# Lag kernels of a state-space phase laid out by DMA within SBUF, into two buffers, instead of through DRAM

## The reference

```python
def step(h, u_blk):
    bu = jnp.einsum('btgn,gpn->btgp', u_blk.astype(jnp.complex64), bbar)
    bu = bu.at[:, 0].add(abar[None] * h)
    a = jnp.broadcast_to(abar, bu.shape)
    _, hs = lax.associative_scan(_linrec_combine, (a, bu), axis=1)
    y = jnp.einsum('btgp,gnp->btgn', hs, cmat).real
    return hs[:, -1], y
...
y = d * u                      # and, for rev in (0, 1): y = y + y_dir
g = jax.nn.gelu(y); out = g * sigmoid(g @ w + bias)
```

## Time and profile before

| | |
|---|---|
| median of 3 runs | 1737.36 us (1733.51 to 1750.48) |
| the profiled execution, its own time | 1738.68 us |
| its span in the profile | 1736.9 us |
| PE busy | 1546.6 us, 89% of the span |
| PE busy, 560 to 920 us | 291.1 of 360 us |
| PE busy, 1200 to 1737 us | 511.4 of 537 us |

### The profile page before, as it was taken

How to read it: one execution, slowest core, us unless ns; L and a number is a source line. 1 busy time by engine, 2 the same in 40 slices (tenths; PEclk the granted TensorE clock), 3 DMA queues, 4 the chain that set the end, 5 groups by cost and what they waited for, 6 DMA issues and landing times. The chain is left out here.

```text
span 1736.9 us, 28020 instructions
## 1 busy us (share of the span) xinstructions
PE 1546.6 (89%) x11286; PEld 1321.5 (76%) x11286; DVE 981.4 (57%) x1271; ACT 806.1 (46%) x1096; POOL 661.2 (38%) x507
## 2 busy tenths in 40 slices
PE   4799999799698899888658988888999999899998
PEld 0378888588687788778648976677999967689997
DVE  6444522488745277755724646564766655556665
ACT  2422222455413577665454434554554454455452
POOL 0088887599798924563741013311000010110000
PEclk8889999999899999887878999998999999899999
DMA  9966666355535677776657455314544333245541
GB/s 390 425 245 226 225 228 250 131 195 188 216 110 202 158 241 217 240 222 173 188 131 277 161 193 207 146 49 153 207 198 193 145 112 145 89 155 218 200 162 49
DMA packets 118713, 332.72 MB, mean 192 GB/s; under 512 B 30772, under 2 KB 72116, under 8 KB 102344
## 3 DMA queue, kind: packets, MB, share of 16 engines
q1 hardware_dynamic: 115734, 305.63, 49.8%
q10 hardware_dynamic: 2868, 25.54, 4.1%
HBM read 290.55 MB, written 40.58 MB: 191 GB/s over the span
## 5 line engine op out<-in xcount | busy, mean ns | idle before, releaser
L3018 PE MATMUL ffn_ps<-ffn_x_lead,w_lead 128*128 128x256 f32 x672 | 188.5, 280 | 1.1 <-DVE w_rest L3097 1.1
L3018 PE MATMUL ffn_ps<-ffn_x_lead,w_rest 128*128 128x256 f32 x672 | 188.7, 281 | 0.0
L3018 PE MATMUL ffn_ps<-ffn_x_rest,w_lead 128*128 128x256 f32 x672 | 188.5, 281 | 0.0
L401 POOL TENSOR_TENSOR w_rest<-resident_ring,w_lead 128x2048 fp32r<-128x2048 f32 x7 | 32.1, 4579 | 396.5 <-ACT w_lead L397 206.3
L3097 DVE TENSOR_TENSOR w_rest<-resident_ring,w_lead 128x2048 fp32r<-128x2048 f32 x42 | 96.1, 2292 | 83.7 <-ACT w_lead L3062 83.7
L365 PE MATMUL qkvz_ps<-qkvz_w_lead,h_lead 128*128 128x512 f32 x320 | 125.9, 393 | 5.4 <-POOL h_rest L646 5.4
L3018 PEld LDWEIGHTS ffn_ps<-ffn_x_lead,w_lead 128*128 128x128 f32 x672 | 126.2, 188 | 2.2 <-issue 1.5
L3018 PEld LDWEIGHTS ffn_ps<-ffn_x_rest,w_lead 128*128 128x128 f32 x672 | 126.5, 188 | 0.7
L3018 PEld LDWEIGHTS ffn_ps<-ffn_x_lead,w_rest 128*128 128x128 f32 x672 | 126.3, 188 | 0.0
L365 PE MATMUL qkvz_ps<-qkvz_w_lead,h_rest 128*128 128x512 f32 x320 | 125.5, 392 | 0.0
L365 PE MATMUL qkvz_ps<-qkvz_w_rest,h_lead 128*128 128x512 f32 x320 | 125.5, 392 | 0.0
(11 more groups left out here) (518 smaller groups left out, 4526.0 us busy)
## 6 DMA issues: line engine op xcount, KB each, us to landing
resident_ring<-in_ffn_gu SPq DMA_DIRECT2D x22, 2048.0 KB, 9.0
ffn_wd<-in_ffn_down SPq DMA_DIRECT2D x22, 1024.0 KB, 4.8
resident_ring<-in_ada_w SPq DMA_DIRECT2D x8, 2048.0 KB, 13.8
xc<-s_q_scratch SPq DMA_DIRECT2D x128, 128.0 KB
resident_x<-in_s_bT SPq DMA_DIRECT2D x64, 256.0 KB
resident_ring<-in_attn_w_in ACTq DMA_DIRECT2D x8, 2048.0 KB, 10.5
s_W_scratch<-resident_x SPq DMA_DIRECT2D x64, 256.0 KB, 3.3
resident_ring<-in_s_w SPq DMA_DIRECT2D x32, 512.0 KB, 8.3
```

Of the source, the lines that this page charges most:

```text
L401: self.core.nc.gpsimd.tensor_tensor(self.slots[1][0], self._raw(r), self.slots[0][0].bitcast(F32), ALU.subtract).then_inc(self.rest_made, 1)
L3018: last = nc.tensor.matmul(ps[s][f][:, m, :], w_part[w][m][:, k, f * P:(f + 1) * P], x_part[x][:, k, :], start=(k, w, x) == (0, 0, 0), stop ...
```

## The change

- `lags` no longer goes to DRAM. ACT, right behind its lag copy and a wait for its completion, issues four DMAs from SBUF to SBUF, one for each `j` (a 32-partition row of groups), which read the windows out of `lags` and write `T`. For tile 0 it waits there for the spill of `x` and the transposes that read `core.x`; for tiles from 2 on it waits for `outputs(kl-2)`.
- `T` has two buffers, `core.x` half and a new `T_odd`. The lag copy waits for the landing of the tile before's windows, as `lags` is single.
- The windows want (channel, step) order in the partitions of `T`. So `us` is stored without a permutation, `ub` is loaded in (channel, step) order, and the rows of `s5_W` follow: the access patterns of L1383 and L1385 swap the two.
- `b_fw`, `b_bw` and `direct` go. `lag_kernels` reads the half of the partitions of `b_all` and `V` that it needs, all backward products first, then the middle ones, then, behind a wait for the backward ones (`behind_done`), the forward ones.
- SP's list is reordered: the load of `ub` with its wait for the store comes early in the turn, the loads of weight tiles behind it.

```diff
@@ InputWeights.load
-                         ap=[[2 * P, CH], [0, SG], [1, 2 * P]]
+                         ap=[[0, SG], [2 * P, CH], [1, 2 * P]]
-                         ap=[[0, CH], [SN * 2 * P, SG], [1, WB * 2 * P]]
+                         ap=[[SN * 2 * P, SG], [0, CH], [1, WB * 2 * P]]
@@ s5_mixer
-        T = core.x[:, 0, :].rearrange("p (j m q) -> p j m q", j=4, q=2)
+        T_odd = ph.sb("T_odd", [P, DM])
+        T_raw = [m.rearrange("p (j m) -> p j m", j=4) for m in (core.x[:, 0, :], T_odd[:])]
+        T = [m.rearrange("p j (m q) -> p j m q", q=2) for m in T_raw]
-            return bass.AP(tensor=lagged.tensor, offset=lagged.offset + k * 2 * SG * CG * LAGW, ap=[[2 * SG, CH], [2 * LAGW, SG * 4], [1, 2 * P]])
+        def shifted(j):
+            return bass.AP(tensor=lags_at.tensor, offset=lags_at.offset + 32 * j * 2 * LAGW, ap=[[2 * LAGW, SG], [2 * SG, CH], [1, 2 * P]])
@@ SP
-                        sp.dma_start(bass.AP(tensor=to.tensor, offset=to.offset, ap=[[CH * NCH, CG], [CG * CH * NCH, SG], [1, CH * NCH]]), us[(n - 1) % 2][:]).then_inc(u_stored[(n - 1) % 2], 16)
+                        sp.dma_start(d["u"][n - 1], us[(n - 1) % 2][:].rearrange("p t n -> p (t n)")).then_inc(u_stored[(n - 1) % 2], 16)
-                        sp.wait_ge(l_kept, kl + 1)
-                        sp.dma_start(bass.AP(tensor=of.tensor, offset=of.offset, ap=[[LAGW * 2, 4], [4 * LAGW * 2, 2 * SG], [1, LAGW * 2]]),
-                                     lags[:].rearrange("m w q -> m (w q)")).then_inc(lag_stored, 16)
-                        sp.wait_ge(lag_stored, 16 * (kl + 1))
-                        sp.wait_ge(y_done, kl)
-                        sp.dma_start(core.x[:, 0, :].rearrange("p (j m) -> p j m", j=4), windows(kl)).then_inc(T_landed, 16)
@@ PE, lag_kernels and outputs
-                    pe.wait_ge(b_copied, k + 1)
+                    pe.wait_ge(b_landed[s], 16 * (k // 2 + 1))
-                    pe.wait_ge(T_landed, 16 * (k + 1))
+                    pe.wait_ge(T_landed[k % 2], 64 * (k // 2 + 1))
@@ ACT
                         if kl:
-                            act.wait_ge(lag_stored, 16 * kl)
+                            act.wait_ge(T_landed[(kl - 1) % 2], 64 * ((kl - 1) // 2 + 1))
                         act.wait_ge(l_done, kl + 1)
                         sc.activation(lags[:].rearrange("p w q -> p q w"), ps_l[:], ACT.Copy).then_inc(l_kept, 1)
+                        if kl == 0:
+                            act.wait_ge(spilled, 16)
+                            act.wait_ge(mod.turned, KT)
+                        act.wait_ge(l_kept, kl + 1)
+                        if kl >= 2:
+                            act.wait_ge(y_done, kl - 1)
+                        for j in range(4):
+                            act.dma_start(T_raw[kl % 2][:, j], shifted(j)).then_inc(T_landed[kl % 2], 16)
-                            direct(m)
-                    if 2 <= kl + 1 < CT:
-                        direct(kl + 1)
```

More of the change, by code:

```diff
@@ L1548, in s5_mixer @@
         ptab = ph.sb("ptab", [P, 2, CH, 2, QG])
-        b_all, b_fw, b_bw = [ph.sb(n, [P, 2, 2, CPAD]) for n in ("b_all", "b_fw", "b_bw")]
+        b_all = ph.sb("b_all", [P, 2, 2, CPAD])
         cc = ph.sb("cc", [P, 4, 2, P])
@@ L1569, in s5_mixer @@
         y_done, y_kept, turned, g_made, cleared, feed_made = [sem(n) for n in "y_done y_kept turned g_made cleared feed_made".split()]
-        lag_stored, T_landed, g_stored, z_stored, feed_in = [sem(n) for n in "lag_stored T_landed g_stored z_stored feed_in".split()]
+        g_stored, z_stored, feed_in = [sem(n) for n in "g_stored z_stored feed_in".split()]
+        T_landed = [sem(f"T_landed{s}") for s in range(2)]
         ub_landed = [sem(f"ub_landed{s}") for s in range(3)]
@@ L1574, in s5_mixer @@
         c_landed, V_landed = [[sem(f"{n}{s}") for s in range(4)] for n in ("c_landed", "V_landed")]
-        b_copied = sem("b_copied")
+        behind_done = sem("behind_done")
         LOADED = EarlyQuads.TILES
@@ L1714, in _ @@
                 g = nc.gpsimd
-                for b in (b_all, b_fw, b_bw):
-                    g.memset(b[:], 0.0).then_inc(cleared, 1)
+                g.memset(b_all[:], 0.0).then_inc(cleared, 1)
                 mod.rests(pool)
@@ L1770, in lag_kernels @@
                         pe.wait_ge(feed_made, 1)
+                    out = lambda j, q, cols: ps_l[32 * j:32 * j + 32, q, cols]
+                    at = lambda j, q: slice((4 * q + j) * SG, (4 * q + j) * SG + 32)
                     for q in range(2):
-                        r = 2 * k + q
-                        out = lambda j, cols: ps_l[32 * j:32 * j + 32, q, cols]
-                        at = lambda j: slice((4 * q + j) * SG, (4 * q + j) * SG + 32)
                         for c in range(2):
                             for j in range(4):
-                                nc.tensor.matmul(out(j, slice(0, P - SG)), b_bw[:, s, c, at(j)], V[:, r % RING, c, j, SG:P], start=c == 0, stop=c == 1)
+                                last = nc.tensor.matmul(out(j, q, slice(0, P - SG)), b_all[hi, s, c, at(j, q)], V[hi, (2 * k + q) % RING, c, j, SG:P], start=c == 0, stop=c == 1)
+                    last.then_inc(behind_done, 1)
+                    for q in range(2):
                         for c in range(2):
@@ L1780, in lag_kernels @@
                                 cols = slice((4 * q + j) * SG, (4 * q + j + 1) * SG)
-                                nc.tensor.matmul(out(j, slice(P - SG, P)), b_all[:, s, c, at(j)], cn[:, s, cols] if c else cc[:, k % 4, 0, cols], start=c == 0, stop=False)
+                                nc.tensor.matmul(out(j, q, slice(P - SG, P)), b_all[:, s, c, at(j, q)], cn[:, s, cols] if c else cc[:, k % 4, 0, cols], start=c == 0, stop=False)
                         for j in range(4):
-                            nc.tensor.matmul(out(j, slice(P - SG, P)), core.ident[:, 32 * j:32 * j + 32], feed[:, r, :], start=False, stop=True)
+                            nc.tensor.matmul(out(j, q, slice(P - SG, P)), core.ident[:, 32 * j:32 * j + 32], feed[:, 2 * k + q, :], start=False, stop=True)
+                    pe.wait_ge(behind_done, k + 1)
+                    for q in range(2):
                         for c in range(2):
                             for j in range(4):
-                                last = nc.tensor.matmul(out(j, slice(P, LAGW)), b_fw[:, s, c, at(j)], V[:, r % RING, c, j, 0:P - SG], start=c == 0, stop=c == 1)
+                                last = nc.tensor.matmul(out(j, q, slice(P, LAGW)), b_all[lo, s, c, at(j, q)], V[lo, (2 * k + q) % RING, c, j, 0:P - SG], start=c == 0, stop=c == 1)
                     last.then_inc(l_done, 1)
@@ L1800, in outputs @@
                                 lhs = ul[:, k % 9, 4 * q + j, :] if src == 2 else hs[:, src, (r % 8) * 4 + j, :]
-                                rhs = T[:, j, :, q] if src == 2 else V[:, r % RING, src, j, :]
+                                rhs = T[k % 2][:, j, :, q] if src == 2 else V[:, r % RING, src, j, :]
                                 last = nc.tensor.matmul(bank[32 * j:32 * j + 32, slot, :], lhs, rhs, start=src == 0, stop=src == 2)
```

60 lines of the change are left out of this document (21 added, 39 removed).

## The result

| | before | after |
|---|---|---|
| median | 1741.69 us (15 runs, 1733.51 to 1753.73) | 1730.08 us (15 runs, 1720.71 to 1740.32) |
| ratio | | 0.9936, 95% interval 0.9917 to 0.9956 |
| the profiled execution, span | 1736.9 us, clock 0.943 | 1734.7 us, clock 0.932 |

The change takes 11 us, 0.6%, where 32 were forecast; the time lies outside the forecast range. In the two profiled executions the state-space phase, from PE's first work in it to the first gate product, went from 364.0 to 353.1 us, 10.9 less. From O(0) to O(15) it was 248.25 - 234.33 = 13.9 less, where the prediction had 31.9. Outside the phase only the two loads for `s5_W` differ, but single executions differ there by some us with the granted clock: the profiled one took 1381.6 us outside the phase, the one before 1372.9.

What follows compares the result with a forecast made beforehand. Two alternating chains were taken to hold PE: T (lag copy, store, load, outputs) and POOL's V. Gains of 7.9 + 12.6 + 0.5 + 10.9 + 0.5 = 32.4 us gave 1705 us, range 1698 to 1713.

Steps and rivals of the forecast that it cites:

- O(0) to O(15): From the start of outputs(0) to that of outputs(15), L(k) being the start of lag_kernels(k): about 216 us instead of 248.25.
- POOL or ACT takes over at once: Rival: with T's waits removed, POOL's or ACT's work holds PE instead; gain 17 to 20 us, chance 0.17.
- O(0) to O(2): Start of outputs(0) to start of outputs(2): nothing gained from 30.3 us, as lag_kernels(3) waits for POOL's V(3).
- O(2) to O(4): Start of outputs(2) to start of outputs(4): 7.9 us less, from 35.9 to 28.0, with POOL's V(5) next to bind.
- O(4) to O(8): Start of outputs(4) to start of outputs(8): 12.6 us less, T's 6.68 us wait and 5.95 us of slower clock.
- O(8) to O(10): Start of outputs(8) to start of outputs(10): nothing gained, as lag_kernels(11) waits for POOL's V(11) and T isn't in this chain.
- O(10) to L(15): Start of outputs(10) to start of lag_kernels(15): 0.5 us less despite 6.29 us of T wait, as POOL makes V(13) to V(15).
- L(15) to O(15): Last tile, lag kernels to outputs: 10.9 us less, from 21.68 to 10.8 (copy 4.3, completion 0.1, issues 2.4, landing 4.0).
- O(6) to O(7): Start of outputs(6) to start of outputs(7): 6.68 us of idle time taken off 20.04, leaving 13.4 us of work.
- Under the 15.1 us that the turns above average: ACT's work per turn with the four issues was put at 13.2 us, under the 15.1 us average turn.
- the slower case: Rival: ACT's issues block, setting the pace from 1.4 us each; 1746 us at 2.0 each, 1773 at 2.5; chance 0.06.
- The attention phase's 0.5 us: Before the state-space phase: loads for `s5_W` landing sooner take 0 to 1.4 us off the attention phase, 0.5 claimed.

Runs made afterwards that it cites:

- filler: The changed kernel with eight useless PE products ahead of the wait for V of tiles 3, 11, 13 and 15; ratio 0.9889.
- issues_behind_and_filler: The changed kernel with ACT's four issues behind its copies into `hs`, and eight useless PE products ahead of V of tiles 3, 11, 13, 15; ratio 0.9846.
- sp_issues: The changed kernel with a tile's four DMAs issued by SP, behind its store of `us`, instead of by ACT; ratio 0.9923.
- odd_tiles_early: The changed kernel with ACT's issues behind its copies into `hs` and V of tiles 5, 7, 9, 11, 13 made early instead of 4, 6, 8, 10, 12; ratio 0.9821.
- via_dram: The changed kernel with T again through DRAM, by a store and four loads on SP, all else as changed; ratio 0.9950.
- both kernels with short V: The kernel before and the changed kernel, each with two of POOL's three operations per half of V left out; ratios 0.9982 and 0.9845.
- new_lag_kernels_alone: The kernel before with only the changed lag kernels, without `b_fw`, `b_bw` and their copies; ratio 1.0021.
- project_first: The changed kernel with PE's projection ahead of the lag kernels, and ACT's lag copy and issues moved back too; ratio 0.9992.
- changed_odd_tiles: The changed kernel with V of tiles 5, 7, 9, 11, 13 made a phase early instead of 4, 6, 8, 10, 12; ratio 0.9910.

## Why the prediction was wrong

The mechanism named first was right, the amount was not, and the rival "POOL or ACT takes over at once" is what happened; it was given a gain of 17 to 20 us, and 11 came.

| step | forecast | measured |
|---|---|---|
| O(0) to O(2) | 0 | +3.2 |
| O(2) to O(4) | -7.9 | -4.7 |
| O(4) to O(8) | -12.6 | -7.1 |
| O(8) to O(10) | 0 | +2.7 |
| O(10) to L(15) | -0.5 | -0.7 |
| L(15) to O(15) | -10.9 | -7.3 |
| sum | -31.9 | -13.9 |

- **The step that failed** is how the gaps of POOL were priced: at their length, with full-clock work behind them ("behind it come lag kernels and a projection, at most 8.0 us"). POOL's end was met to 0.1 us: O(2) to L(5) was 721.84 - 701.70 = 20.14 us against 20.1. From L(5) to O(4) it was 11.03 against 7.9. The same stretch behind L(3) is 11.55 where it was 7.9 before, behind L(6) 11.75 where it was 9.3, behind L(11) 9.5 where it was 6.5, ahead of O(7) 1.5 more, and L(15)'s copy came 7.66 instead of 4.3 us behind L(15) (3.4 more). Together 3.1 + 3.7 + 2.4 + 3.0 + 1.5 + 3.4 = 17 of the 18 us that are missing, but not all of it behind POOL: L(3), L(5), L(11) and 1.1 us at L(15) make 11; L(6) and O(7) (4 us) stand behind waits for ACT (3.70 us ahead of the transposes, 2.48 for `zb`), which weren't priced either; and 2.25 us at L(15) are idle time within it (below). Some 0.2 of each stretch with lag kernels is their slower form. The prediction took the slow clock off with T's waits (5.95 us between O(7) and O(8), which went: 24.14 to 18.18) and didn't bring it in again with POOL's. filler shows that the clock is worth this at L(11), where it was kept at 1.00: L(11) to O(10) is 5.40 us instead of 9.49 (6.53 before, with a part of it at the lower clock). At L(3) it is 8.04 us instead of 11.55 in issues_behind_and_filler, where 1.17 us of idle time stand behind the products without use. L(5) got no such products in any run, but in sp_issues, where its gap is 0.69 us instead of 1.70, it is 8.01 us instead of 11.03.
- **O(8) to O(10), O(0) to O(2)**: "T isn't in this chain" was right, and both still got longer by that clock.
- **O(6) to O(7)**: -2.5 instead of -6.68, since a half projection waited 2.48 us for `zb`, which ACT made at 779.02 behind copies that its issues had put off. In sp_issues, where ACT issues nothing, that wait is gone and O(6) to O(7) is 13.50 us, as forecast (13.4). "Under the 15.1 us that the turns above average" held for the sum of ACT's work and missed its order.
- **The last tile**: 14.4 us against 10.8. Copy 7.7 against 4.3 (the clock, and 2.25 us of idle time within L(15)), issues 3.4 against 2.5, landing 3.35 behind the last issue against 4.0. The idle time has no semaphore in the trace, but it has a pattern: in six kernels PE stands 1.2 to 2.7 us ahead of the last six products of L(15), and each time a packet of the DMA queue that the profile calls "instruction" has ended 1.2 to 1.4 us before PE goes on (the change: 892.2 to 893.1, PE at 894.50; odd_tiles_early: 873.7 to 874.7, PE at 876.11). In sp_issues, via_dram, filler and both kernels with short V that packet comes earlier against the products, and there is no gap. That PE waited for its own instructions there is a guess that fits; which engine's they were isn't shown. The Trainium skill, "SBUF — State Buffer", section on Door 1, has 104 GB/s for the first 16 partitions. By that figure the 512 KB would take an estimated 5.0 us. From the first issue to O(15) it was 6.7 us, half of it issues, and only the first of the four DMAs reads the first 16 partitions, so the figure was neither confirmed nor refuted.
- **Right**: the waits of T ahead of O(3), O(7), O(11) are gone; L(3), L(5), L(11), L(15) wait for POOL (and L(13), not foreseen); O(8) waits 4.61 us for its states; O(10) to L(15), the trap, gave 0.7 us; no wait for `ub`. O(12) waited 3.18 us, under the 4 foreseen. ACT's four issues together took at most 5.24 us in a turn, 1.3 each, under the 1.4 (its x) from which the slower case was to set the pace.
- **Not right among the signs**: the clock in 664 to 730 was to be above 0.9 and was 0.87, as before, since it stayed low behind L(3) and L(5).
- **The attention phase's 0.5 us** can't be seen: PE starts the state-space phase 2.4 us later, behind unchanged products at a lower clock.

Open: why the whole times of some kernels differ by 7 to 10 us from what their O(0) to O(15) gives (new_lag_kernels_alone, project_first, changed_odd_tiles, sp_issues). Where the clock behind the phase was low it explains a part, but one profiled execution each is too little, and in new_lag_kernels_alone and sp_issues it wasn't low. Open too is what makes the instruction packet late at L(15).
